# A second place for the broadcast query row, a new order of one queue's loads, and four small moves in a decoder layer

## What is computed

```
xn  = rmsnorm(x) * (1 + scale) + shift            # adaLN
z   = xn @ w_in                                   # q, k, v, recurrent q, f, i, og, and two gates ga, gb
# for each sample, attention over the cache:
s_past = einsum('bqhcd,bkhcd->bhcqk', q, k_past) * scale
p      = softmax(s)[:, :, 0] - lam * softmax(s)[:, :, 1]
o      = p @ v_past + p_new @ v
# for each sample, one step of the recurrence:
S = exp(g)[..., None] * S + k[..., None] * v[..., None, :]
o = einsum('bhk,bhkv->bhv', q, S)
# merge of the two branches, output product, residual, then the gated MLP with a width-3 convolution
```

## Time and profile before

| | |
|---|---|
| median of three runs | 2263.7 us |
| the profiled execution's own time | 2261.58 us |
| its span | 2259.8 us |
| mean granted clock of PE | 0.997 |
| PE busy | 2224.5 us, 98% of the span |
| DVE, ACT, POOL busy | 1544.4, 1140.7, 955.0 us |
| gates stage, 1090 to 1265 us: DMA share, moved | 0.90, 334 GB/s |

### The profile page before, as it was taken

How to read it: one execution, slowest core, us unless ns; L and a number is a source line. 1 busy time by engine, 2 the same in 40 slices (tenths; PEclk the granted TensorE clock), 3 DMA queues, 4 the chain that set the end, 5 groups by cost and what they waited for, 6 DMA issues and landing times. The chain is left out here.

```text
span 2259.8 us, 47757 instructions
## 1 busy us (share of the span) xinstructions
PE 2224.5 (98%) x18881; PEld 2106.5 (93%) x18881; DVE 1544.4 (68%) x2534; ACT 1140.7 (50%) x2343; POOL 955.0 (42%) x1149
## 2 busy tenths in 40 slices
PE   7999999999999999999999999999999999999999
PEld 5899999989999999989887899999999999999999
DVE  5668677777777686776687515416988888876535
ACT  6566666666666666655433402015466666643110
POOL 1135262634444452625443314442155656535431
PEclk9999999999999999999999999999999999999999
DMA  7212122131213131221699713111355454485212
GB/s 301 91 55 94 46 84 66 58 105 56 98 51 103 45 100 48 78 75 40 249 349 344 280 41 122 48 42 59 132 192 188 183 187 180 183 304 198 89 47 94
DMA packets 103513, 288.34 MB, mean 128 GB/s; under 512 B 18426, under 2 KB 26490, under 8 KB 103290
## 3 DMA queue, kind: packets, MB, share of 16 engines
q1 hardware_dynamic: 102138, 281.09, 35.3%
q10 hardware_dynamic: 1152, 4.19, 0.5%
HBM read 213.18 MB, written 63.77 MB: 123 GB/s over the span
## 5 line engine op out<-in xcount | busy, mean ns | idle before, releaser
L172 PE MATMUL h_G<-xn_hi,h_w_hi 128*128 128x344 f32 x1368 | 457.4, 334 | 0.2 <-ACT h_d_oraw L918 0.2
L172 PE MATMUL h_G<-xn_hi,h_w_lo 128*128 128x344 f32 x1368 | 437.0, 319 | 0.0
L172 PE MATMUL h_G<-xn_lo,h_w_hi 128*128 128x344 f32 x1368 | 436.6, 319 | 0.0
L1203 POOL TENSOR_TENSOR h_w_lo<-h_w_raw,h_w_hi 128x1024 fp32r<-128x1024 f32 x58 | 149.2, 2573 | 367.6 <-ACT h_w_hi L780 332.0
L172 PEld LDWEIGHTS h_G<-xn_hi,h_w_hi 128*128 128x128 f32 x1368 | 258.3, 189 | 32.5 <-issue 21.2
L172 PEld LDWEIGHTS h_G<-xn_lo,h_w_hi 128*128 128x128 f32 x1368 | 257.1, 188 | 4.6
L172 PEld LDWEIGHTS h_G<-xn_hi,h_w_lo 128*128 128x128 f32 x1368 | 257.1, 188 | 0.0
L3095 DVE SCALAR_TENSOR_TENSOR x<-t_ps,keep_mod,x 128x344 f32<-128x344 f32 x168 | 94.3, 571 | 163.6 <-PE t_ps L2923 100.9
L2923 PE MATMUL t_ps<-f_act_lo,f_d_hi 128*128 128x344 f32 x528 | 169.4, 321 | 0.0
L2923 PE MATMUL t_ps<-f_act_hi,f_d_lo 128*128 128x344 f32 x528 | 168.8, 320 | 0.0
L2923 PE MATMUL t_ps<-f_act_hi,f_d_hi 128*128 128x344 f32 x528 | 168.5, 319 | 0.1
(11 more groups left out here) (467 smaller groups left out, 6998.1 us busy)
## 6 DMA issues: line engine op xcount, KB each, us to landing
h_w_raw<-in_w_in SPq DMA_DIRECT2D x72, 512.0 KB, 3.7
y_rows<-f_y SPq DMA_DIRECT2D x44, 516.0 KB, 2.7
f_y_pair<-y_rows SPq DMA_DIRECT2D x22, 1032.0 KB, 5.2
h_d_ada_w<-in_w_ada SPq DMA_DIRECT2D x32, 512.0 KB, 4.2
g_kp<-in_cache_k SPq DMA_DIRECT2D x32, 512.0 KB, 6.9
g_vp<-in_cache_v SPq DMA_DIRECT2D x32, 512.0 KB, 5.5
f_a<-in_w_ffn SPq DMA_DIRECT2D x57, 256.0 KB, 2.6
h_w_raw<-in_w_mix SPq DMA_DIRECT2D x24, 512.0 KB, 3.5
```

Source lines behind the costliest of these rows:

```text
L172: ins = eng.matmul(out, w[:, k * P:(k + 1) * P], x[:, k, columns], start=(k == 0 and n == 0), stop=(k == n_k - 1 and n == 2))
L1203: pool.tensor_tensor(wlo[w][:, :], raw[r][:, :], whi[w][:, :].bitcast(F32), ALU.subtract).then_inc(lo_done.sem, 1)
```

## The change

In the gates stage the query row gets a second place, the last tile of `gate[1]` (`gate[1][:, 7, 0:D]`), which is written as a gate only at the end; samples alternate between the two. The query row of sample i+2 is loaded behind the last key page of sample i+1. The state of sample i, from i = 1 on, is loaded behind key pages 0 and 1 of sample i+1, and no longer behind the value row; its wait goes with it.

The four small moves: (1) `split(2)` of the norm stage stands behind row k = 1; (2) in the heads stage PE's wait for the ones stands behind the first sums; (3) the two sample blocks of the last head are turned, and copied by ACT, behind the pieces of k = 1; (4) the split of the first branch row (k = 0) is made at the end of the gates stage in place of the start of the tail; for that one gate tile more (`gate_a`, the 11th) is finished by ACT in the tail.

```diff
-        qB, vB = row("qB"), row("vB")
+        qB, vB = [row("qB"), gate[1][:, H - 1, 0:D]], row("vB")
...
             load_pages(0)
+            load_spread(1)
             m = 3
+            def next_state(i):
+                sp.wait_ge(st_out.sem, st_out.at(i - 1, 1))
+                sp.wait_ge(rec_out.sem, rec_out.at(i - 1, 1))
+                load_state(i)
             for i in range(NS):
                 for j in range(PAGES):
+                    if i and j == 2:
+                        next_state(i)
                     sp.wait_ge(k_summed.sem, k_summed.at(i, j + 1))
                     if i + 1 < NS:
-                        if j == 2:
-                            sp.wait_ge(k_scaled.sem, k_scaled.at(i, 2))
-                            load_spread(i + 1)
                         load_keys(i + 1, j)
+                if i + 2 < NS:
+                    sp.wait_ge(k_scaled.sem, k_scaled.at(i, 2))
+                    load_spread(i + 2)
...
                     load_values(i + 1)
-                if i + 1 < NS:
-                    sp.wait_ge(st_out.sem, st_out.at(i, 1))
-                    sp.wait_ge(rec_out.sem, rec_out.at(i, 1))
-                    load_state(i + 1)
                 sp.wait_ge(pv.sem, pv.at(i, 1))
...
# ACT, gates stage
-                    for t in range(cut_tiles(NS - 1).stop, N_TILES - 1):
+                    act.wait_ge(oa_in.sem, oa_in.at(KT, 0))
+                    act.wait_ge(row_free.sem, 1)
+                    for j in range(NP):
+                        if j == NP - 1:
+                            act.wait_ge(samples_in.sem, 1)
+                        act.activation(oh[:, 0, cols(j)], x1[:, 0, cols(j)], ACT.Copy).then_inc(row_hi.sem, 1)
+                    for t in range(cut_tiles(NS - 1).stop, N_TILES - 2):
...
# DVE, gates stage, last
+            for j in range(NP):
+                dve.wait_ge(row_hi.sem, j + 1)
+                ch(dve.tensor_tensor(ol[:, 0, cols(j)], x1[:, 0, cols(j)], oh[:, 0, cols(j)].bitcast(F32), ALU.subtract))
...
# norm stage, ACT
+                if k == 1:
+                    split(2)
...
-                if k == KT // 2:
-                    split(2)
...
# heads stage, PE
-            pe.wait_ge(ones_ready.sem, 1)
             late_value(0)
...
             late_value(2)
+            pe.wait_ge(ones_ready.sem, 1)
```

More of the change, by code:

```diff
@@ L163, in __call__, with product @@
         return t
-def product(eng, out, whi, wlo, xhi, xlo, n_k, columns, between=None):
+def product(eng, out, whi, wlo, xhi, xlo, n_k, columns, between=None, first=None):
     for k in range(n_k):
@@ L173, in product @@
                              start=(k == 0 and n == 0), stop=(k == n_k - 1 and n == 2))
+        if k == 0 and first is not None:
+            ins.then_inc(first.sem, 1)
     return ins
@@ L995, in _ @@
                         piece(h, n)
+                    if k == 1 and no_next(h):
+                        act.wait_ge(rows_turned.sem, 1)
+                        act.activation(rows[:, :, :], X[0:H * NS, 0, 0:2 * P].rearrange("p (a b) -> p a b", a=2), ACT.Copy).then_inc(rows_ready.sem, 1)
                     act.wait_ge(os_done.sem, os_done.at(h, k + 1))
@@ L1166, in _ @@
                     pe.transpose(kht_ps, K[:, 0, :], ident[:, :]).then_inc(rec_done.sem, 1)
[L1167 to L1172, removed]
                     if k < 6 and not no_next(h):
@@ L1179, in _ @@
                         piece(h, n, (SUMS_BEHIND, attention_sums, h) if k == SUMS_AT else None)
+                    if k == 1 and no_next(h):
+                        pe.wait_ge(sample_qkv.sem, sample_qkv.at(h, 1))
+                        pe.wait_ge(sample_rec.sem, sample_rec.at(h, 1))
+                        for n, src in enumerate((c["s_q"], c["s_ib"])):
+                            ins = pe.transpose(X[0:H * NS, 0, n * P:(n + 1) * P], src[:, :, :].rearrange("p h n -> p (h n)"), ident[:, :])
+                        ins.then_inc(rows_turned.sem, 1)
                     pe.wait_ge(at_ready.sem, at_ready.at(h, k + 1))
@@ L1531, with gates_stage @@
 IN_SET = NS // SETS
-def gates_stage(nc, a, o, c, d, xh, xl, gate, slots, x1, third):
+def gates_stage(nc, a, o, c, d, xh, xl, gate, slots, x1, third, oh, ol):
     with Stage(c) as ctx:
@@ L1571, in gates_stage @@
         k_in = [S(f"k_in{i}", step=16) for i in range(PAGES)]
-        q_in, vb_in, v_in = S("q_in", step=16), S("v_rows_in", step=16), S("v_in", PAGES, step=16)
+        q_in = [S(f"q_in{i}", step=16) for i in range(2)]
+        vb_in, v_in = S("v_rows_in", step=16), S("v_in", PAGES, step=16)
         st_in, st_out = S("st_in", step=16), S("st_out", step=16)
@@ L1763, in piece @@
                     pe.wait_ge(free.sem, free.at(n - PIECE_BANKS + 1, 0))
-                product(pe, ps[:, n % PIECE_BANKS, 0:TH], whi[buf(m)], wlo[buf(m)], xh, xl, KT, cols(j)).then_inc(done.sem, 1)
+                product(pe, ps[:, n % PIECE_BANKS, 0:TH], whi[buf(m)], wlo[buf(m)], xh, xl, KT, cols(j),
+                        first=row_free if n == N_PIECES - 1 else None).then_inc(done.sem, 1)
             def new_scores():
@@ L2544, in high @@
             def high(n):
-                for k in range(KT):
+                for k in range(n == 0, KT):
                     branch_in(act, n, k)
[L2547 to L2551, removed]
-                        ins.then_inc(o_hi.sem, 1)
-                    else:
-                        act.activation(oh[:, k, :], x[:, k, :], ACT.Copy).then_inc(o_hi.sem, 1)
+                    act.activation(oh[:, k, :], x[:, k, :], ACT.Copy).then_inc(o_hi.sem, 1)
+            for sig, n in ((first_hi, NP - 1), (o_hi, 1)):
+                act.sem_inc(sig.sem, n)
             high(0)
-            g = gate[1][:, H - 1, :]
             act.wait_ge(gate_cut.sem, 1)
-            ch(act.activation(g, g, ACT.Ln))
-            ch.sync()
-            act.activation(g, g, ACT.Exp, scale=-1.0).then_inc(gate_ready.sem, 1)
+            for half in gate:
+                g = half[:, H - 1, :]
+                ch(act.activation(g, g, ACT.Ln))
+                ch.sync()
+                act.activation(g, g, ACT.Exp, scale=-1.0).then_inc(gate_ready.sem, 1)
             def square(t):
@@ L2807, in by_tiles @@
                     for j in range(NP):
-                        if n == 0 and k == 0 and j < NP - 1:
-                            pe.wait_ge(first_hi.sem, j + 1)
-                            pe.wait_ge(first_lo.sem, j + 1)
-                        elif n is not None and (j == 0 or k == 0 and n == 0):
+                        if n is not None and j == 0:
                             pe.wait_ge(o_hi.sem, o_hi.at(n * KT + k + 1, 0))
@@ L3149, in norm @@
                         rest(j, k - 1)
-            low(0, range(KT))
+            for sig, n in ((first_lo, NP - 1), (o_lo, 1)):
+                dve.sem_inc(sig.sem, n)
+            low(0, range(1, KT))
             dve.wait_ge(o_lo.sem, KT)
```

41 lines of the change are left out of this document (15 added, 26 removed).

## The result

The changed kernel takes 2285.12 us (median of six runs, 2280.8 to 2286.21) against 2263.43 us before; the ratio is 1.0097, with a 95% interval of 1.0086 to 1.0108. Slower by 21.7 us, where +5.7 was forecast, and above the end of the range (2281). The profiled execution has a span of 2282.7 us, 22.9 more than before.

The account below looks back on a forecast made before the run. PE, 98% busy, was taken as the bound. 2261.58 + 8.9 (gates stage) - 0.65 - 0.1 - 0.6 - 1.85 gave 2267.3 us profiled, 2269.4 as a median (+5.7); range 2252 to 2281.

Parts of the forecast that it names:

- The query row's wait goes: Gates stage: DVE's six waits for the query row, 11.7 us, go; DVE would be 3 us or more ahead of PE.
- the five terms of that 7.2: Gates stage, if pages meet no DVE operation: five turn intervals lose waits of 0.3, 1.1, 0.3, 3.5 and 2.0 us.
- POOL's multiplies come early and meet DVE's operations: Gates stage: POOL's key multiplies start 4 to 9 us behind turns, each blocking DVE's state operations or cut for 2.38 us.
- The 7.2 us for six intervals: Gates stage, turns 1 to 7: net change of 2.0, 1.5, 0.7, 2.0, -1.1 and 2.1 us, clock not included.
- the prediction's own lower bound: Gates stage: if the pages meet no DVE operation, the waits simply go, -7.2 us.
- the far bound: Gates stage: both POOL multiplies between state operations, value product waits 3.1 to 3.4 us, clock falls again, about +21 us.
- when the state lands: Gates stage: the state's wait ends 16.8 us behind the previous turn, some 2.4 us before the next one.
- The late state: Rival, chance 0.08: state behind two key pages lands late in the gates stage, PE loses 12.6 us in seven samples, 2273.
- collision: Main case, chance 0.47: POOL's key multiplies block DVE in the gates stage; 2269.4 us, own range 2262 to 2281.
- The clock: Gates stage: PE idles 5.6 us before turn 7, its clock falls behind it, +1.7 us.
- The small moves: Outside the sample loop: norm stage 0.65, heads stage 0.1 and 0.6, start of the tail 1.85 us gained.

Follow-up runs that it names:

- the second experiment: The changed kernel with the state's load put back behind the value row; two places for the query row and the small moves stay: 2255.33 us, ratio 0.9964.
- the first: The kernel before with the four small moves alone, query row and state loaded as before: 2259.98 us, ratio 0.9988.
- the thin run: The changed kernel with POOL's two key multiplies per sample cut to 128 of 1024 columns: 2269.84 us, ratio 1.0031.
- the thin runs: The changed kernel with POOL's key multiplies cut to 128 columns, 2269.84 us; the same with the state's load ahead of all key pages, 2253.0 us.
- the held runs: The changed kernel with POOL held until DVE's first sum, 2269.16 us; with the state ahead of all key pages, 2256.49 held and 2268.07 not held.

## Why the prediction was wrong

*The query row's wait goes.* Right: no wait of DVE for it is left. Its worth, in the second experiment against the first, is 4.7 us, where DVE's chain without waits gave 7.2 at most. Two of the five terms of that 7.2, 0.3 each, do not come out of the rows: interval 2 to 3 lies 0.9 us over the floor, and the chain that was worked out for it, 16.2 us, is well under it.

*POOL's multiplies come early and meet DVE's operations.* Right in mechanism and place, and taken alone nearly right in size. They start 6.5 to 9.5 us behind turns 1 to 6, close to the 4 to 9 that I had said, and L1977 takes 3.3 us in place of 1.2. The 7.2 us for six intervals are what is left of the collisions when the waits that go are taken off, 7.2 us by the prediction's own lower bound; so it had 14.4 us for the collisions, and the pairs of runs say 11.6 to 15.9. The run with the state ahead of the key pages is about the case that the sum describes: 2268.1 us, where 2269.4 was forecast, and 128.1 us from turn 1 to turn 7, where 129.5 was forecast and 122.4 was measured before. A part of this agreement is luck: its single intervals are up to 1.4 us longer (the first) and up to 2.3 us shorter (the last) than forecast. In the single operation the count was low: I had the two key multiplies, and half a blocked operation for the weight subtraction, but all three block whole; behind turn 3 they push DVE back 2.04, 1.96 and 2.16 us, 6.2 in place of 5.4. The prediction also spoke of two-input operations, while its first row for it, the cut (2.69 us in place of 0.69), reads one tile; the rows here show both kinds blocked. And I took DVE's end alone as what sets the interval, leaving the value product's wait to the far bound.

*The step that failed: when the state lands.* The prediction put the state's issue at the moment when the old state has left, 16.8 us behind the previous turn, as in the earlier trace rows, with the key pages 2 and 3 behind it. That was true of before, where the value pages stood behind the state. I read the diff as a move of the state past key pages 0 and 1; it is also a move past four value pages, and past the wait for PE's value product ahead of them. So what comes last at that place is no longer the state's way out (0.8 us of waiting) but PE's value product and six transfers, 6.0 us from the first to the state; and the landing takes 6.8 us, where it took 3.5 at the old place. The prediction expected the state some 1 to 2 us behind the turn; it was there 5.1 to 6.9 us behind turns 1 to 6. That is the whole miss: 17.0 us between the two places of the load, where the result lies 15.7 above the forecast.

The late state was a rival of 0.08 with a price of 12.6 us and a point of decision of 5.2 us behind the turn. Its chance was wrong. The point fits: in the run with POOL held until the new state, DVE begins to scale the state 5.40 us behind turn 2 and the value product starts 9.38 us behind it, hardly past the 9.3 at which it is wanted. The price is near the 12.7 to 17.0 us of the runs, but in part by luck. By the rival's own rule, what the landing lies past 5.2 us, the thin run (6.1 to 7.3 us behind turns 1 to 6) would lose an estimated 9 us, and it loses 16.8. What makes up the rest was not taken apart; the blocked L1969 at turns 1 and 4 is in it.

*Rivals taken as alternatives.* Late state and collision were weighed as two cases, 2269 and 2273, and the range ended at 2281. They come from one cause, SP's new order, so they come together and add: by the thin runs 2253.0 with neither, 2268.1 and 2269.8 with one, 2285.1 with both, where the two single prices would give 2284.9. By the held runs (2256.5, 2268.1, 2269.2) both together cost 4.3 us more than the single prices.

*The clock.* The loss of 1.7 us behind turn 7 came about, with 5.49 us of idle time before it, 5.6 forecast. That the two agree is luck: the interval was 23.8 us and not 21.0, with 2.64 us of its waiting at the value product; in the run with the state first the wait before turn 7 is 3.1 us. The granted clock of the stretch, the column behind PE's busy time, is below full:

```profile
1272.00:1298.00 26.00, 24.52 (x157) 0.93 0.66 237
```

From turn 7 to the tail's first matmul the sum would be 26.34, less 0.92 for the shorter wait there (1.96 to 1.04), and 1.65 for the clock: 27.07; it is 26.79. The clock also fell four times between turns 1 and 5, which I had for the far bound only.

*The small moves.* 3.2 us forecast, 2.7 measured, inside the interval. Single ones, by the traces: the wait at L385 in the norm stage fell from 1.85 to 0.84 plus 0.19; at the heads' start 0.90 us stay, now put down to PE's own sequencer, so 0 of 0.1; L1171's 0.6 is gone; in the tail the first wait is 1.04 us, where a start at 1275.6 would have left 0.86, and the trace puts it down to the barrier (DVEq L3156), not to a load or a split; the second is 0.70, 0.9 forecast:

```profile
1300.27 0.40 PE L2828 MATMUL t_ps<-branch_hi,h_w_hi 128*128 128x344 f32 x1 [1.04 <-DVEq L3156]
...
1302.61 0.39 PE L2828 MATMUL t_ps<-branch_hi,h_w_hi 128*128 128x344 f32 x1 [0.70 <-DVE branch_lo L3072]
```

The matmuls between are at full clock, as forecast, and the start costs 1.74 us in two waits in place of 1.96 and a fallen clock.

## What to carry to other kernels

When a load moves in a queue's list, write down everything it is now behind, with the wait of each, and ask again which of them ends last: a wait that was the longest at the old place may be nothing at the new one. When one engine's operations block another's, as POOL's do DVE's here, freeing one earlier can land its work on the other's critical operations; delay it to where the other does reductions rather than only past the operation that was seen to suffer. And cases with one common cause are not alternatives: their prices add.

## What was not expected of the hardware

After 7.54 us of idle time PE's clock was down with the first matmul (16 in 3.64 us, as against 1.92). After 3.32 us of idle time before turn 6 in the trace before, the matmuls of the next piece first ran 0.16 us apart, and 0.29 apart from 1.1 us behind the turn on. The length of the idle time alone does not tell whether the clock falls: in the changed kernel it fell behind 1.93 us (the first of these rows, 16 matmuls in 3.09 us) and not behind 2.64 (the second, 1.92 us).

```profile
1166.85 3.09 PE L1818 MATMUL g_V<-g_vp,g_pt 128*32 128x512 f32 x16 [1.93 <-DVE g_pt L1980]
...
1261.67 1.92 PE L1818 MATMUL g_V<-g_vp,g_pt 128*32 128x512 f32 x16 [2.64 <-DVE g_pt L1980]
```

And the size of a transfer does not tell its landing: 512 KB of state landed in 3.5 us at the old place, where SP had waited for the old state just before, and in 6.8 us behind six others of the same size. With only the four value pages ahead it was still 6.5 us (median, the run with the state ahead of all key pages), so the count of transfers ahead is not the measure either. The state on its way out landed in 7.9 us before and in 4.7 us in the changed order; what it met there before was not tried.

```profile
out_s_state<-g_st ACTq DMA_DIRECT2D x5, 512.0 KB, 4.7
```
